# First chunk of every linear part: products issued one kind at a time over all tickets, instead of ticket by ticket

## The reference

```
f = _conv_ffn(_modulate(x, ml[3], ml[4]), ffn_w_in[i], ffn_conv_w[i], ffn_conv_b[i], ffn_w_out[i])
...
def _conv_ffn(h, w_in, conv_w, conv_b, w_out):
    gate, up = jnp.split(h @ w_in, 2, axis=-1)
    return (jax.nn.silu(_dwconv(gate, conv_w, conv_b)) * up) @ w_out
```

## Time and profile before

| what | value |
|---|---|
| median of 3 runs | 2425.54 us (2423.97 to 2426.81) |
| profiled execution, its own time | 2416.99 us |
| its span | 2415.2 us |
| TensorE busy | 2307.4 us, 96% of the span |
| VectorE, ScalarE busy | 1350.2 us (56%), 1215.5 us (50%) |
| mean granted TensorE clock | 0.997 of 2.4 GHz |
| HBM read | 309.10 MB, 128 GB/s over the span |

### The profile page before, as it was taken

How to read it: one execution, slowest core, us unless ns; L and a number is a source line. 1 busy time by engine, 2 the same in 40 slices (tenths; PEclk the granted TensorE clock), 3 DMA queues, 4 the chain that set the end, 5 groups by cost and what they waited for, 6 DMA issues and landing times.

```text
span 2415.2 us, 34444 instructions
## 1 busy us (share of the span) xinstructions
PE 2307.4 (96%) x13798; PEld 1903.9 (79%) x13798; DVE 1350.2 (56%) x2358; ACT 1215.5 (50%) x2163; POOL 0.2 (0%) x4
## 2 busy tenths in 40 slices
PE   7999999999999999999999999999999998899998
PEld 7758999966999876788676776877777876668898
DVE  4656655565665665445555654356665445546664
ACT  5555644555554474444343343247555335546764
POOL 0000000000000000000000000000000000000000
PEclk9999999999999999999999999999999999999999
DMA  7782555684455322222121211222222322214442
GB/s 258 300 293 90 190 175 175 231 320 166 159 181 185 122 88 74 97 91 88 69 73 53 74 64 53 87 70 88 94 98 87 105 88 83 92 36 143 172 157 105
DMA packets 45419, 312.32 MB, mean 129 GB/s; under 512 B 4775, under 2 KB 6951, under 8 KB 8276
## 3 DMA queue, kind: packets, MB, share of 16 engines
q1 hardware_dynamic: 45268, 310.19, 36.5%
HBM read 309.10 MB, written 1.07 MB: 128 GB/s over the span
## 4 chain that ended last, share of the span: by engine, by line
PE 84%; DVE 8%; ACT 6%; issue 2%; DMA 0%; SPq 0%; ACTq 0%; DVEq 0%
PE bank L670 57%; PE bank L675 8%; DVE ws L1508 3%; ACT ws L1096 2%; PE bank L851 2%; PE bank L987 2%; PE bank L742 1%; PE bank L753 1%; DVE xs L1524 1%; PE bank L893 1%; PE bank L858 1%; PE bank L957 1%; PE bank L969 1%; PE bank L835 1%; PE bank L834 1%
## 5 line engine op out<-in xcount | busy, mean ns | idle before, releaser
L670 PE MATMUL bank<-xs,ws 128*128 128x256 f32 (+1 forms) x9648 | 1563.3, 324 | 55.1 <-DVE xs L1524 31.4
L670 PEld LDWEIGHTS bank<-xs,ws 128*128 128x128 f32 x9648 | 1398.2, 191 | 223.3 <-DVE xs L1524 45.3
L1508 DVE TENSOR_TENSOR ws<-ring,ws 128x1024 fp32r<-128x1024 f32 x464 | 547.8, 1222 | 293.5 <-ACT ws L1096 293.2
L1096 ACT ACTIVATE ws<-ring 128x1024 fp32r<-128x1024 f32 x464 | 464.6, 1049 | 288.0 <-PE bank L670 275.1
L1524 DVE TENSOR_TENSOR xs<-arena,xs 128x512 fp32r<-128x512 f32 (+1 forms) x286 | 162.0, 582 | 309.8 <-ACT xs L1112 309.1
L1112 ACT ACTIVATE xs<-arena 128x512 fp32r<-128x512 f32 (+1 forms) x286 | 148.9, 538 | 332.3 <-PE bank L670 217.8
L1112 ACT ACTIVATE xs<-hT 128x256 fp32r<-128x256 f32 (+1 forms) x328 | 165.4, 517 | 236.7 <-PE bank L670 204.7
L1524 DVE TENSOR_TENSOR xs<-hT,xs 128x256 fp32r<-128x256 f32 (+1 forms) x328 | 178.0, 552 | 189.1 <-ACT xs L1112 188.8
L675 PE MATMUL bank<-ws,xs 128*128 128x512 f32 (+1 forms) x1008 | 229.9, 388 | 9.3 <-DVE xs L1524 5.2
L675 PEld LDWEIGHTS bank<-ws,xs 128*128 128x128 f32 x1008 | 188.4, 189 | 49.6 <-DVE xs L1524 6.5
L742 PE MATMUL bank<-con 128*128 128x256 f32 (+1 forms) x282 | 59.8, 363 | 2.2 <-DVE arena L2009 2.2
(11 more groups left out here) (245 smaller groups left out, 1543.9 us busy)
## 6 DMA issues: line engine op xcount, KB each, us to landing
ring<-in_stream SPq DMA_DIRECT2D x233, 1024.0 KB, 4.8
arena<-in_side SPq DMA_DIRECT2D x56, 1024.0 KB, 6.4
arena<-in_tokens SPq DMA_DIRECT2D x1, 2048.0 KB, 11.1
arena<-bias_vectors SPq DMA_DIRECT2D x1, 1536.0 KB, 7.2
out<-arena SPq DMA_DIRECT2D x2, 512.0 KB, 3.1
arena<-in_params SPq DMA_DIRECT2D x1, 918.0 KB, 6.8
arena<-bias_vectors SPq DMA_DIRECT2D x1, 706.0 KB, 8.7
con<-in_consts SPq DMA_DIRECT2D x1, 449.5 KB, 3.4
```

What stands on the lines that cost most here:

```text
L670: ins = mm(ps(n, 0, g.T), a[wi][:, p * P:(p + 1) * P], x[xi], start=first, stop=last)
L1096: do(ws[:, i % 2, 0, c], ring[:, w % R, c], ACT.Copy).then_inc(w_high, 1)
L1508: ins = v.tensor_tensor(ws[:, i % 2, 1, c], ring[:, w % R, c], ws[:, i % 2, 0, c].bitcast(F32), ALU.subtract)
```

## The change

In every group that has more than two chunks and is not of the `natural` form (input as the stationary operand: `nat`, `m_v`, `a_v`), the first chunk is issued in three passes. The first pass does high by high for all tickets and waits for `w_high` (both halves of the slot's copy), `x_high` and the banks. The second does high weights by low input after `x_done`. The third does low weights by high input after `slot_done`. Later chunks are as before. 53 groups take the new path. The number of matmuls, and the programs of the other engines, stay the same.

```
+                    a = [ws[:, (g.s0 + k // g.kc) % 2, i, j * cols:(j + 1) * cols] for i in range(2)]
+                    x = [split_x(q, i) for i in range(2)]
+                    if k == 0 and g.K > 2 and not g.natural:
+
+                        pe.wait_ge(w_high, 2 * g.s0 + 2)
+                        pe.wait_ge(x_high, q + 1)
+                        for p in range(g.tickets):
+                            n = N0 + p
+                            if n >= BANKS:
+                                pe.wait_ge(bank_free[n % BANKS], n // BANKS)
+                            mm(ps(n, 0, g.T), a[0][:, p * P:(p + 1) * P], x[0], start=True, stop=False)
+                        pe.wait_ge(x_done, q + 1)
+                        for p in range(g.tickets):
+                            mm(ps(N0 + p, 0, g.T), a[0][:, p * P:(p + 1) * P], x[1], start=False, stop=False)
+                        pe.wait_ge(slot_done, w + 1)
+                        for p in range(g.tickets):
+                            ins = mm(ps(N0 + p, 0, g.T), a[1][:, p * P:(p + 1) * P], x[0], start=False, stop=False)
+                        ins.then_inc(chunk_done, 1)
+                        continue
                     if j == 0:
                         pe.wait_ge(slot_done, w + 1)
                     pe.wait_ge(x_done, q + 1)
```

More of the change, by code:

```diff
@@ L655, in linear @@
                     w, j, q = g.w0 + k // g.kc, k % g.kc, g.q0 + k
+                    cols = SLOT // g.kc
+                    a = [ws[:, (g.s0 + k // g.kc) % 2, i, j * cols:(j + 1) * cols] for i in range(2)]
[16 more added lines that the diff above has]
+                        continue
                     if j == 0:
@@ L658, in linear @@
                     pe.wait_ge(x_done, q + 1)
-                    cols = SLOT // g.kc
-                    a = [ws[:, (g.s0 + k // g.kc) % 2, i, j * cols:(j + 1) * cols] for i in range(2)]
-                    x = [split_x(q, i) for i in range(2)]
                     for p in range(g.tickets):
```

## The result

The changed kernel takes 2437.02 us (median of 8 runs, 2435.5 to 2438.46) against 2422.11 us of the kernel before (8 runs, 2415.62 to 2426.81): the ratio is 1.0062, with a 95% interval of 1.0051 to 1.0074. That is 15 us slower, clear of noise, and inside the range. The profiled execution took 2435.81 us.

The account below looks back on a forecast made before the run. TensorE, busy 96% of the span, was taken to bound the kernel. Bank losses of 15.2 us less gains of 5.2 gave 10, clock falls added 5; 15 us on the median made 2440.5 us, range 2431 to 2448.

Parts of the forecast that it names:

- The hidden first passes: At starts where the input's low half is late, the first pass runs before it: gains 1.0, 3.0, 0.9, 0.1 us.
- Gains given back: m_up(0), ffn_in(0, 0), a_dkv start 0.7 to 0.9 us earlier but wait longer at the third chunk: 0.2 us together.
- The late banks: In out, m_qk(0), ffn_out(0), ffn_in(1, 0 to 4), ffn_out(1), late banks delay the first chunk: losses 15.2 us.
- the waits that I named as signs: Waits of 2.5 us in ffn_in(1, 1 to 4), 1.7 us twice for line 1134, 2.6 us at ffn_out(0).
- The eight starts of proj(l, 1) and up: In proj(l, 1) and up(l, 1 to 3), the eighth bank is free 0.25 us before it is due: loss 0.
- The clock: Behind lengthened stands TensorE's granted clock falls three or four times, 1.5 us each: 5 us more, ends 0 and 11.
- the six stands: TensorE's stands in ffn_in(1, 1 to 4), ffn_out(0) and ffn_out(1), growing to some 3.5, 2.9 and 2.6 us.
- The fall from which I took the price: Behind the 2.64 us gap before a_dkv, the clock fell for 3.41 us; cost up to 1.8 us, taken as 1.5.
- The step from the profiled execution to the median: The median lay 8.5 us above the profiled execution; the change was taken not to affect this, so 15 us was added.
- only the banks: Rival: late banks cost time but the clock stays, 2435.5 us; chance 0.2.
- The clock falls behind every stand: Rival: falls behind all stands, 10 + 9 to 11 us, 2445 us; chance 0.15.
- Faster: Rival: first passes are hidden and bank waits don't grow, since emptyings come earlier; 2420.3 us, chance 0.04.

Follow-up runs that it names:

- early-only: The kernel before, with the three passes only in the groups whose banks are free in time: 2415.39 us, ratio 0.9974.
- filled kernel: The changed kernel with 5 matmuls without use in each stand of ffn_in(1, 1 to 4) and ffn_out(1): 2428.48 us, ratio 1.0029.
- second new trace of before: The kernel before, unchanged, profiled once more in another execution: 2424.48 us.
- two other traces of before: The kernel before, unchanged, profiled in two further executions: 2422.4 and 2424.48 us.
- the trace of before: The kernel before, unchanged, in the profiled execution that the prediction rests on: 2416.99 us.
- the two chunks by halves: The kernel before, with the first two chunks of ffn_in(1, 1 to 4) and ffn_out(1) issued together by halves of the tickets: 2410.20 us, ratio 0.9952.
- late-only: The kernel before, with the three passes only in out, m_qk(0), ffn_out(0), ffn_in(1, 0 to 4) and ffn_out(1): 2444.18 us, ratio 1.0090.
- the one that empties first: The changed kernel, with ScalarE emptying all the last group's tickets in ffn_in(1, 1 to 5) before its copies: 2420.28 us, ratio 1.0001.
- both filled ones: The changed kernel with matmuls without use in five stands, 20 per stand (2454.52 us) or 5 per stand (2428.48 us).

## Why the prediction was right, point by point

- *The hidden first passes.* Right in place and size. Measured against the end of the input's low half, the first chunk ends 0.98 us earlier in proj(0, 0) (predicted 1.0), 0.52 to 0.54 in the five starts of up, down and proj(1, 0) (0.5), 0.92 in m_out (0.9).
- *Gains given back.* Right in kind. m_up(0) starts 0.79 us earlier and loses all of it at its third chunk; ffn_in(0, 0) and a_dkv likewise. The 0.2 us that I left for the three was 0.
- *The late banks.* Right, and the waits that I named as signs came: 2.40 us at the fifth ticket in ffn_in(1, 1), 1.6 twice for the `dfn` bank, 2.47 in ffn_out(0). Loss of the first chunk: out 1.67 each (predicted 1.6), m_qk(0) 1.06 (1.0), ffn_out(0) 3.0 (2.9). ffn_in(1, 1) became 3.11 us longer, of which 1.49 is the price of a fall in the early-only trace, which leaves 1.62 (1.6); in the filled kernel, with no fall there, it is 1.60. ffn_out(1): 3.1 with a fall, 1.59 without, in the filled kernel (1.6). The eight starts of proj(l, 1) and up that had 0.25 us to spare kept their 2.88 us.
- *The clock.* The kind is right, the count was low. I expected three or four falls behind the six stands, 5 us; the profile has six stretches of 3.41 us behind five of them, and none behind ffn_out(0). They cost 8.1 us, 1.35 each. The two profiled executions lie 18.8 us apart, and laid over each other this is late banks 15.5 (predicted 15.2), gains of the starts 5.0 (5.2), these falls 8.1 (5), and 0.2 at other places: 1.1 more from a_dkv to a_out, where the clock falls at other points, 0.4 less in ffn_in(1, 5) and 0.5 less at the first transfers. The fall from which I took the price, at the gap of the earlier trace rows, cost nothing where it stood: the second new trace of before has none there and its a_dkv is as long, because TensorE waits 1.06 us for the third chunk's input there instead. In a stretch full of matmuls 1.5 is right all the same.
- *The step from the profiled execution to the median.* The prediction said that nothing in the change bears on the 8.5 us between the two. That was wrong, and the 8.5 itself did not hold. The median of three runs was 3.4 us above that of eight, 2422.11, which is 5.1 above the profiled execution. And that execution has no fall behind the stands which the change lengthens, while the two other traces of before have one and two, 1.5 and 3.0 us. An ordinary run of before has thus paid for some of the falls already, and the change makes nearly sure what was chance. It costs 14.9 us at the median and 18.8 between the profiled executions. The falls already paid for go the right way and are of this size; that they are the whole difference is not shown. The low count and this step cancel, so that 15 was predicted and 15 measured is in part luck: against its own base, the trace of before, the sum was 3.8 us short.
- *The rivals.* By the number alone "only the banks" was not excluded: its 2435.5 us is nearer to 2437.0 than my 2440.5, since both started from the median of three. The filled kernel excludes it: with the falls behind the stands gone the time would have been 2428.5. "The clock falls behind every stand", to which I gave 0.15, is in mechanism the nearer one: falls behind five stands of six, though for 8.1 us and not 9 to 11. "Faster" needed ScalarE to empty the banks earlier; moved there by hand, it takes back 15 to 17 us and ends at the time of before (1.0001), since out, m_qk(0), ffn_out(0) and ffn_out(1) still lose.

## What to carry to other kernels

An order that goes over all results once per kind of product asks for every output buffer within the first third of the work. It pays where an operand is late and costs where a buffer is: before regrouping, find out for each start which of the two comes last. If the last of n buffers is late in both orders, the price is the work that the new order puts behind it, here 14 matmuls, 1.6 us. Where buffers are late, go the other way and do more of the contracted dimension on the buffers that are free, as the two chunks by halves do; where operands are late and buffers free, the passes by kind are right, and both can stand in one kernel. And look for longer matmuls behind each stand of TensorE: a short stand can cost more in clock than in waiting.

## What the runs showed of the hardware

- The clock falls behind quite short stands, and not in every execution. Behind the stand of 1.44 or 1.45 us in ffn_in(1, 1) the granted clock fell in three of the traces (early-only and both new ones of before) and stayed at 1.00 in the trace of before. Behind the four stands of 2.40 to 2.54 us in ffn_in(1, 1 to 4) it fell every time, in the changed kernel and in the late-only one.
- A longer stand is no surer sign. Behind one of 2.33 us in ffn_out(1) the clock fell in those two kernels and not in the one that empties first; behind one of 2.47 us in ffn_out(0) it fell in the late-only kernel and in both filled ones, where it cost 1.6 us more, and not in the changed kernel; behind one of 3.46 us in a_dq it stayed at 1.00 in the trace of before and fell in both new ones.
- A fall lasts 3.4 us here and costs 1.5 us of a stretch full of matmuls, and nothing in a_dkv, where without it TensorE stands for an input instead.
- The spread of the kernel before goes with the clock: its runs with a mean granted clock of 0.997 took 2415.7 to 2418.0 us, those at 0.993 to 0.994 took 2422.2 to 2425.0. Two executions of the same kernel can so differ by 8 us and more with no instruction changed, and the profile that the prediction rests on lay 5.1 us below the median of eight runs.
- Matmuls without use in a stand held the clock up, 2.32 us of them per stand, and gave back about 8 us although they do no work.
